# Ten dense projection tiles of each layer as three products of rounded parts, with VectorE making their low weights and GpSimd the activations' low parts

## The reference, cut to what matters

```python
h = rms_norm(x, norm1_g[l])          # 256 x 1024
p = h @ w_in[l]                      # columns: stick q k v | RWKV | MoBA q k v | HGRN q f i g | four gates of 1024
...
x = x + mixers_gated_and_projected
x = x + (silu(h2 @ w_ffn_gate) * (h2 @ w_ffn_up)) @ w_ffn_down
```

## Time and profile before

| what | us |
|---|---|
| three runs | 1962.47, 1962.41, 1956.23 (median 1962.41) |
| profiled execution | 1960.12 |
| its span | 1957.2 |
| TensorE busy | 1748.5 |
| VectorE busy | 804.1 |
| ScalarE busy | 606.2 |
| GpSimd busy | 141.7 |

### The profile page before, as it was taken

How to read it: one execution, slowest core, us unless ns; L and a number is a source line. 1 busy time by engine, 2 the same in 40 slices (tenths; PEclk the granted TensorE clock), 3 DMA queues, 4 the chain that set the end, 5 groups by cost and what they waited for, 6 DMA issues and landing times.

```text
span 1957.2 us, 27219 instructions
## 1 busy us (share of the span) xinstructions
PE 1748.5 (89%) x11670; PEld 1387.5 (71%) x11670; DVE 804.1 (41%) x1271; ACT 606.2 (31%) x873; POOL 141.7 (7%) x86
## 2 busy tenths in 40 slices
PE   7999989999999999899999999999998975666655
PEld 6899878888898899788999998567987321211111
DVE  4345664555535434665566675343446100000001
ACT  3322441443343223440544464542442100000001
POOL 0043100100000144000100020000000000000000
PEclk9999988999999999998999999999999988778778
DMA  5322422687752323334644422402129999999997
GB/s 225 127 97 86 142 96 99 224 335 311 287 199 68 127 87 112 105 130 159 259 173 162 162 108 70 165 8 86 44 89 429 398 428 427 427 428 428 427 428 321
DMA packets 34536, 414.92 MB, mean 212 GB/s; under 512 B 3824, under 2 KB 4080, under 8 KB 4720
## 3 DMA queue, kind: packets, MB, share of 16 engines
q1 hardware_dynamic: 33984, 410.63, 53.3%
q10 hardware_dynamic: 432, 2.56, 0.3%
HBM read 412.13 MB, written 1.05 MB: 211 GB/s over the span
## 4 chain that ended last, share of the span: by engine, by line
PE 72%; DMA 16%; DVE 5%; ACT 4%; another core or an unknown queue 2%; issue 1%; POOL 0%; SPq 0%; DVEq 0%; ACTq 0%
PE ps L212 52%; DMA high<-in_w_e_up_dram 8%; PE ps L743 7%; DMA high<-in_w_e_gate_dram 5%; PE ps L1540 4%; PE ps L1168 3%; DMA high<-in_w_e_down_dram 3%; DVE high L171 2%; PE ps L1140 2%; ACT high L206 2%; PE ps L782 1%; DMA low<-in_late_dram 1%; PE ps L739 1%; PE ps L1557 1%
## 5 line engine op out<-in xcount | busy, mean ns | idle before, releaser
L212 PEld LDWEIGHTS ps<-rarena 128*128 128x128 f32 x3648 | 447.5, 192 | 16.1 <-DVE low L171 7.8
L212 PE MATMUL ps<-rarena 128*128 128x256 f32 (+1 forms) x3648 | 457.6, 287 | 0.0
L206 ACT ACTIVATE high<-ps 128x256 f32<-128x256 f32 (+2 forms) x188 | 90.9, 484 | 528.3 <-PE ps L1540 193.0
L212 PE MATMUL ps<-rarena,rring 128*128 128x256 f32 x1728 | 231.9, 289 | 3.3 <-DVE rring L171 2.8
L212 PEld LDWEIGHTS ps<-rarena,rring 128*128 128x128 f32 x1728 | 215.0, 192 | 8.3 <-DVE rring L171 3.6
L206 ACT ACTIVATE rarena<-ring 128x2048 fp32r<-128x2048 f32 x76 | 140.4, 1848 | 246.8 <-PE ps L212 187.7
L171 DVE TENSOR_TENSOR rarena<-ring,rarena 128x2048 fp32r<-128x2048 f32 x76 | 168.9, 2223 | 107.2 <-ACT rarena L206 105.8
L212 PE MATMUL ps<-high,ring 128*128 128x256 f32 (+1 forms) x864 | 205.9, 390 | 2.8 <-ACT low L206 2.8
L212 PEld LDWEIGHTS ps<-high,ring 128*128 128x128 f32 x864 | 161.5, 190 | 38.5 <-issue 15.9
L171 DVE TENSOR_TENSOR high<-high,ps 128x512 f32<-128x512 f32 x52 | 35.7, 687 | 295.6 <-PE ps L1540 251.3
L1540 PE MATMUL ps<-high,low 128*32 128x512 f32 x560 | 86.5, 748 | 48.1 <-DMA high<-in_w_e_up_dram 29.2
(11 more groups left out here) (205 smaller groups left out, 1762.1 us busy)
## 6 DMA issues: line engine op xcount, KB each, us to landing
ring<-in_w_in_dram SPq DMA_DIRECT2D x56, 1024.0 KB, 4.9
ring<-in_w_ffn_up_dram SPq DMA_DIRECT2D x22, 2048.0 KB, 9.1
high<-in_w_e_down_dram SPq DMA_DIRECT2D x19, 2048.0 KB, 50.3
high<-in_w_e_up_dram SPq DMA_DIRECT2D x18, 2048.0 KB, 49.6
high<-in_w_e_gate_dram SPq DMA_DIRECT2D x17, 2048.0 KB, 47.2
ring<-in_w_mod_dram SPq DMA_DIRECT2D x12, 2048.0 KB, 7.9
ring<-in_w_in_dram SPq DMA_DIRECT2D x10, 2048.0 KB, 7.8
ring<-in_w_e_up_dram SPq DMA_DIRECT2D x9, 2048.0 KB, 49.5
```

The source lines that it names most:

```text
L206: return self.e.activation(out, x, f, scale=scale, **kw)
L212: ins = self.e.matmul(out, l, r, start=first and i == 0, stop=end and i == n - 1)
```

## The change

Units 2 to 11 are made of rounded parts like those behind them. ScalarE rounds the weights of units 2 to 5 ahead of the mixer, right behind the normalized tiles, and of 6 to 11 two units ahead of the use. VectorE makes the low weights of units 2 to 11, two units ahead of the use. GpSimd makes the low parts `hl` of the eight normalized tiles in place of VectorE; it still makes the low weights of units 12 to 33. Units 0 and 1 stay dense. Loads, slots and plans stay as they are.

```diff
@@ scalar_program, units(l)
-                    if PARTS_FROM <= u + 2 < PARTS_TO:
+                    if 6 <= u + 2 < PARTS_TO:
                         rounded_ahead(l, u + 2)
@@ scalar_program, for l in range(L)
                     high_part(f"{l}h{n}.hi", B.hh[:, n, :], B.h[:, n, :])
                     if n in EARLY_STEPS[l]:
                         next(rw)
+                for u in range(PARTS_FROM, 6):
+                    rounded_ahead(l, u)
                 fill = [units(l)]
                 mix([rw], fill, RW_PLAN, False)
@@ vector_program, units(l, gates)
-                    if PARTS_ON_V <= u + 2 < PARTS_TO:
+                    if PARTS_FROM <= u + 2 < PARTS_ON_G or PARTS_ON_V <= u + 2 < PARTS_TO:
                         kind, z = UNITS[u + 2][2], UNITS[u + 2][4]
                         if kind == "c" or z == 0:
                             low_weights_of(l, u + 2)
@@ vector_program, for l in range(L)
-                def low_tile(n):
-                    V.wait_ge(f"{l}h{n}.hi")
-                    low_part(B.hl[:, n, :], B.h[:, n, :], B.hh[:, n, :], f"{l}h{n}.lo")
-
                 normed_tile(0)
                 for n, i in enumerate(RP):
                     if n < 7:
                         normed_tile(n + 1)
-                    low_tile(n)
                     V.wait_ge(f"{l}rp{i}.ps")
@@ pool_program, units(l)
-                for u in range(PARTS_FROM, PARTS_ON_V):
+                for n in range(8):
+                    G.wait_ge(f"{l}h{n}.hi")
+                    G.tt(fr(B.hl[:, n, :]), B.h[:, n, :], B.hh[:, n, :], ALU.subtract).then_inc(*G(f"{l}h{n}.lo"))
+                for u in range(PARTS_ON_G, PARTS_ON_V):
@@
-PARTS_FROM, PARTS_ON_V, PARTS_TO, FORGET_FROM = 12, 34, 52, 20
+PARTS_FROM, PARTS_ON_G, PARTS_ON_V, PARTS_TO, FORGET_FROM = 2, 12, 34, 52, 20
```

## The result

The changed kernel takes 1981.29 us (median of four runs, 1979.19 to 1984.49), the kernel before 1962.44 us beside it (four runs). The ratio is 1.0104, 95% interval 1.0078 to 1.0131: 1% slower, and clear of no change. The forecast was 1966.5 us and "same", with a range up to 1975; the time lies 6 us above that range. In the two profiled executions the span went from 1957.2 to 1979.5 us, 22.3 us more.

What follows compares the result with a forecast made beforehand. TensorE was taken to bound the changed tiles' stretch, but waits on VectorE and ScalarE would eat the matmuls' 10.8 us: layer 0 -1.2, layer 1 +2.9, clock +2.4, together +4.1 us, so 1966.5 us, range 1955 to 1975.

Steps and rivals of the forecast that it cites:

- the term of the clock: One fall to 1.2 GHz behind the wait of 3.8 us in each layer, 1.2 us each, 2.4 us in all.
- the access of GpSimd beside VectorE: Eight subtractions a layer moved from VectorE to GpSimd, in the stage of the normalized tiles, costed at nothing.
- the alternating halves: Four half tiles alternating with small products before the first level product: 4 x 0.32 us plus 0.8 to 0.9, 2.2 saved.
- The gain in layer 0: Normalized tiles' stage: TensorE's 2.83 us gap and 1.25 us at the decay product vanish, 4.1 us, layer 0 only.
- The first new wait: Before the bonus product: VectorE's subtractions of tiles 2 to 5 delay the key norm's maximum; TensorE stands 4.6 us.
- The second new wait: Before the keys' transposes: subtractions of tiles 7 and 8 queue ahead of the key products; TensorE idles 3.8 us.
- The first level product: First level product of the RWKV chain: +2.9 us by TensorE and VectorE, near 101.5 us in layer 0, 684.8 in layer 1.
- X1: The first level product in layer 0, at 102.73 us before the change and forecast near 101.5.
- Rival (b): Clock falls follow the waits before bonus product and transposes in both layers, four at 2.3 us: 1973 us; chance 0.33.
- hidden as before: Before the first level product, tile 11 and half of 12 stay hidden behind VectorE's level masks; VectorE keeps up.
- Rival (a): TensorE stays the bound and every saving counts: about 1948 us, near 1955 with one wait left per layer; chance 0.12.

Runs made afterwards that it cites:

- e1: Changed kernel with units 2 to 11 dense, only the normalized tiles' low parts on GpSimd: 1956.68 us, ratio 0.9985 to the kernel before; repeated, 1951.88 us, 0.9952.
- e4: Changed kernel with VectorE's subtractions for units 4, 5 and 8 moved back one unit, behind the chains: 1967.07 us, ratio 1.0042 to the kernel before.
- e2: Changed kernel with unused matmuls added ahead of TensorE's three waits in each layer: 1972.5 us, ratio 1.0059 to the kernel before.
- e3: Changed kernel with unit 14's low weights made by VectorE in place of GpSimd: 1973.09 us, ratio 1.0067 to the kernel before.
- e7: Changed kernel with VectorE's subtractions for units 4, 5 and 8 behind the chains and unit 14's low weights on VectorE: 1959.03 us, ratio 0.999.
- e5: Changed kernel with GpSimd making the low weights of units 2 to 11 as well, VectorE none: 1976.37 us, ratio 1.0085 to the kernel before.
- e9: Changed kernel with units 2 to 7 dense, unit 8's low weights one unit later, 14's on VectorE: 1952.65 us, ratio 0.9951; repeated, 1954.08 us, 0.9961.
- e10: Changed kernel with e7's edits, and ScalarE's roundings of units 4 and 5 behind the key norm's exponential: 1957.64 us, ratio 0.9981 to the kernel before.

## Why the prediction was wrong, point by point

The forecast was +4.1 us on the span, and +22.3 were measured. Of the 18.2 us between them some 9 are the term of the clock (2 x (2.3 + 1.7 + 1.7) in place of 2.4), 4.2 the access of GpSimd beside VectorE that was put at nothing, 2.0 the alternating halves, and 2.7 falls further on. This counts the first fall of layer 1 on the chain like that of layer 0, where two executions show it. The two waits that were worked out from VectorE's queue were right, in place and in length.

**The gain in layer 0** was right: forecast 4.1 us, measured 4.2 us at the start of layer 1 (e1). That the low parts cost nothing on GpSimd held too, though they made VectorE's neighbours slower (0.83 us in place of 0.48 at 26.39), where nothing waited.

**The first new wait** was right: the maximum forecast at 51.6 and measured at 52.09, bonus product near 60 and measured at 60.16, 4.6 us of standing still and measured 3.50 + 1.09. In layer 1 it is 3.13 + 1.12.

**The second new wait** was right: forecast 3.8 us of standing still, measured 3.72 in both layers; the transposes at 76.83 + 6.0 - 4.1 = 78.7 and their second half 0.5 later, measured 79.52 in the execution where the clock did not fall before them. e4 confirms the cause of both.

**The first level product** was forecast at 101.5 and came at 108.77. This is where the forecast failed, by 7.3 us in layer 0, in three steps.

- The term of the clock was mis-sized, and this is most of the error. I took one fall for each layer at 1.2 us, on the ground that the wait of 3.8 us lay between two known gaps and that VectorE would hide half. Measured: three falls a layer. On the chain in layer 0 the first costs 2.26 us (the two executions), the second 1.7, and a third, behind X1, another 1.7. (By e2, which has no fall there, the second costs 1.5: from the transposes to X1 it takes 25.54 us, the changed kernel 26.99.) The wait of 4.6 us I had worked out myself got no fall in my sum, although it was longer than the one that did. What I held against it, that the clock kept up in the gap of 2.9 us at 151.9, was one execution: the same gap has a fall behind it in nine of the fourteen profiles (last section). Rival (b) had this mechanism, four falls at 2.3 us and 1973 us, with a chance of 0.33; it was nearer, and still 8 us short, since it had neither the third wait nor its fall. The Trainium skill ("TensorE: Matmul & The Clock Gate", section "Why this matters for your kernels") asks that idle gaps between bursts of matmuls be avoided, since one takes the clock back to its lower level. The trace agrees for all sixteen waits of 3.71 to 3.74 us in the profiles of these kernels, and not for the one of 3.55 us in the second execution of the changed kernel.
- GpSimd beside the chain was costed at nothing, and the level masks were called "hidden as before". That step failed: the mask takes 2.1 us longer, all of it on the chain, and it lengthens the wait from 1.59 to 3.71 us, with the third fall behind it. e3 shows both. I had looked at GpSimd's own time and at who waits for it, and not at what it does to an instruction that runs beside it. The earlier trace rows could not show it, but the row of GpSimd at 101.97 could: 2.93 us in place of a mean of 2.40.
- The alternating halves were to save 0.5 us each, with the small products gaining as well. Measured from 88.15 to 90.84 is 2.69 us, against 3.00 before: 0.31 each, 1.2 us in place of 2.2. The small product gains nothing: 1.14 us before and after.

Together 2.3 + 1.7 + 2.1 + 1.0 = 7.1 of the 7.3 us. Layer 1 begins 7.6 us later than before, where the forecast had it level (1.2 us earlier, less 1.2 for a fall), and has the same terms again; behind its own three waits the offset is 19.0 us. Of the rest up to 22.3 us, 2.7 are falls of the clock further on in layer 1, 1.55 us at 888 and 2.62 in place of 1.51 at 843; why they shift was not tried. For the last 0.6 us I have no account.

**Rival (a)**, that TensorE stays the bound, is ruled out by the waits themselves, and e7 says more: with all three waits shortened the kernel is where the kernel before was. Two of the waits left are 2.1 and 1.6 us, since the added rounding and subtraction per tile, 1.06 and 1.23 us, lie on engines that the chain needs, and the chain was at TensorE's heels already.

## What to carry to other kernels

When a change trades TensorE's time for work on VectorE and ScalarE inside a dependent chain, write out each engine's queue at the chain's links, and price a new standstill of TensorE at its length plus a fall of the clock (here 1.5 to 2.9 us, behind all but one of 22 waits of 3.1 to 3.7), as the forecast and not as a rival. Before work is put on GpSimd, look at which VectorE instructions that read only SBUF will run at that time: if one is on the chain, its start may wait for the whole GpSimd instruction. And split a change in its parts: here a half that gains 0.15 to 0.5% was buried under one that costs 1.2 to 1.5% (1.0104 against 0.9985 and 0.9952).

## What the runs showed of the hardware

**Operations of VectorE and GpSimd on SBUF exclude each other in these rows, an instruction at a time.** The one that starts first takes its usual time. A VectorE operation with two inputs in SBUF that starts 0.08 us after a GpSimd one of 2.34 us takes 3.34 in place of 1.22; the four that start 0.04 us after two of them take 6.83 in place of 2.60; a GpSimd instruction that starts after VectorE's takes 2.93 in place of 2.4. One tensor input is enough: two operations of one tensor and a column take 4.82 us in place of 0.74 (e5). With an input in PSUM VectorE's time stays at 1.49 us for two. The Trainium skill ("SBUF — State Buffer", section "Terms") describes a pair of ports that one engine holds for its full instruction while the other blocks; the rows agree. That no operation on PSUM suffers was seen for this one form and not tried for others.

**The same gap has a fall behind it in one execution and none in another.** Timelines of TensorE in the changed kernel and in e9, the same place in the code:

```profile
162.42 2.05 PE L743 MATMUL ps<-high 128*128 128x128 f32 x16 [2.97 <-DVE high L171]
```

```profile
150.04 3.65 PE L743 MATMUL ps<-high 128*128 128x128 f32 x16 [2.97 <-DVE high L171]
```

The gap is 2.97 us in both; the sixteen records take 2.05 us at the higher clock and 3.65 at the lower. Over the fourteen profiles, one execution each, the falls behind equal waits of TensorE count so:

| wait, us | where | with a fall |
|---|---|---|
| 3.71 to 3.74 | transposes, X1 | 16 of 16 |
| 3.10 to 3.55 | before unit 3, changed kernel and e3 | 5 of 6 |
| 2.96 to 2.97 | 150 to 162 us, all kernels | 9 of 14 |
| 2.27 to 2.28 | 313 to 326 us (layer 0), all kernels | 14 of 14 |
| 2.09 to 2.11 | transposes, e4, e7 and e10 | 3 of 6 |

So the length of a wait does not decide alone; the one of 2.28 us brings a fall every time and the longer one of 2.97 does not. Nor has a fall one price: behind the 2.28 us gap it cost 6.4 us in the changed kernel (clock 0.52 from 325.5 to 339) and 1.7 us in e9. Falls that come in one execution and not in the next would explain part of why runs of one kernel differ by up to 0.9%; that was argued from these profiles and not tried.
